# The head of a two-block kernel on one core: three units of the first projection multiplied together, their input loaded ahead of the fourth half of weights, squares on ScalarE

## The reference, cut to what matters

```python
def rmsnorm(x, g):
    xf = x.astype(jnp.float32)
    y = xf * lax.rsqrt(jnp.mean(xf * xf, axis=-1, keepdims=True) + EPS)
    return (y * g.astype(jnp.float32)).astype(x.dtype)
...
        z = rmsnorm(h, norm1_g[l])
        proj = z @ w_in[l]
        u_pool = proj[..., :POOL_WIDTH]
        x_lru = proj[..., POOL_WIDTH:POOL_WIDTH + LRU_WIDTH]
        g_lru = proj[..., POOL_WIDTH + LRU_WIDTH:]
```

## Time and profile before

| | before |
|---|---|
| median of 3 runs | 3289.7 us (3287.39 to 3292.03) |
| the profiled execution's own time | 3288.59 us |
| its span, first to last instruction | 3286.8 us |
| TensorE busy | 3185.9 us (97%) |
| VectorE busy | 2188.5 us (67%) |
| ScalarE busy | 1691.0 us (51%) |
| GpSimd busy | 806.1 us (25%) |
| mean granted TensorE clock | 0.988 |

### The profile page before, as it was taken

One profiled execution on the slowest core, in us unless ns is written; L12 is line 12 of the kernel. 1 busy time (PEld: TensorE's weight loads), 2 busy tenths in 40 slices (PEclk: granted clock), 3 DMA queues, 4 the chain that ended last, 5 costly groups with the idle time before them and its releaser, 6 DMA issues.

```text
span 3286.8 us, 46958 instructions
## 1 busy us (share of the span) xinstructions
PE 3185.9 (97%) x18222; PEld 2777.5 (85%) x18222; DVE 2188.5 (67%) x2908; ACT 1691.0 (51%) x2625; POOL 806.1 (25%) x782
## 2 busy tenths in 40 slices
PE   7999989999999999999999998999999899999998
PEld 6788878888888888888888887888888788888887
DVE  7757999864655555555646569999675865555564
ACT  5554457644545444454545655565657444444454
POOL 1332321321312222231313434222351200000003
PEclk9999999999999999999999999999999899999999
DMA  6465546666565656666666554555666466666664
GB/s 213 150 199 180 178 160 221 234 188 212 186 213 187 213 186 212 186 211 186 186 211 186 187 184 141 159 162 175 190 189 189 148 189 189 191 189 190 191 188 140
DMA packets 177709, 615.35 MB, mean 187 GB/s; under 512 B 18128, under 2 KB 34896, under 8 KB 176080
## 3 DMA queue, kind: packets, MB, share of 16 engines
q1 hardware_dynamic: 157824, 572.59, 55.1%
q10 hardware_dynamic: 19664, 39.76, 3.4%
HBM read 593.41 MB, written 18.87 MB: 186 GB/s over the span
## 4 chain that ended last, share of the span: by engine, by line
PE 74%; DVE 15%; issue 4%; ACT 3%; POOL 3%; DMA 1%; ACTq 0%; DVEq 0%; POOLq 0%
PE G L404 49%; PE G L405 25%; DVE lo L1002 6%; DVE CV L1305 2%; POOL tS L1487 1%; DVE oneB L1280 1%; ACT hi L631 1%; DVE oneA L1282 1%; DVE tS L1008 1%; ACT oneB L808 0%; DVE ZA L1328 0%; POOL X L1507 0%; POOL acc L1512 0%; DVE oneB L1285 0%; DMA X<-in_xT 0%
## 5 line engine op out<-in xcount | busy, mean ns | idle before, releaser
L404 PE MATMUL G<-ZA,hi 128*128 128x512 f32 x5120 | 1821.7, 400 | 29.4 <-DVE lo L1002 11.7
L1002 DVE TENSOR_TENSOR lo<-raw,hi 128x1024 fp32r<-128x1024 f32 x1088 | 1436.9, 1342 | 305.5 <-ACT hi L631 305.0
L405 PE MATMUL G<-ZA,lo 128*128 128x256 f32 x5120 | 1437.9, 281 | 0.0
L404 PE MATMUL G<-ZB,hi 128*128 128x512 f32 x3568 | 1250.2, 396 | 5.9 <-DVE ZB L1293 4.9
L404 PEld LDWEIGHTS G<-ZA,hi 128*128 128x128 f32 x5120 | 969.1, 189 | 261.9 <-DVE lo L1002 13.6
L631 ACT ACTIVATE hi<-raw 128x1024 fp32r<-128x1024 f32 x1088 | 1115.5, 1051 | 65.9 <-DMA raw<-in_pv 37.8
L405 PE MATMUL G<-ZB,lo 128*128 128x256 f32 x3584 | 1001.6, 279 | 0.0
L405 PEld LDWEIGHTS G<-ZA,lo 128*128 128x128 f32 x5120 | 973.8, 190 | 0.4
L404 PEld LDWEIGHTS G<-ZB,hi 128*128 128x128 f32 x3568 | 669.6, 188 | 167.5 <-DVE lo L1002 3.3
L638 ACT ACTIVATE tA<-G 128x256 f32<-128x256 f32 x559 | 212.4, 380 | 974.2 <-PE G L405 973.3
L405 PEld LDWEIGHTS G<-ZB,lo 128*128 128x128 f32 x3584 | 676.2, 189 | 0.0
(11 more groups left out here) (270 smaller groups left out, 1363.2 us busy)
## 6 DMA issues: line engine op xcount, KB each, us to landing
raw<-in_pu SPq DMA_DIRECT2D x256, 512.0 KB, 3.6
raw<-in_pv SPq DMA_DIRECT2D x256, 512.0 KB, 3.9
raw<-in_w_in SPq DMA_DIRECT2D x192, 512.0 KB, 3.5
raw<-in_w_up SPq DMA_DIRECT2D x128, 512.0 KB, 3.8
raw<-in_w_down SPq DMA_DIRECT2D x128, 512.0 KB, 4.2
raw<-in_w_out SPq DMA_DIRECT2D x32, 512.0 KB, 3.5
raw<-in_wq SPq DMA_DIRECT2D x32, 512.0 KB, 3.5
g_scratch<-stage ACTq DMA_DIRECT2D x16, 1024.0 KB, 4.8
```

The lines of the kernel that those rows point to most:

```text
L404: pe.matmul(G[:, 0:512], hi[h % NW][:, k % 8, :], Z[:, k, :], start=first, stop=False, skip_group_check=True)
L405: m = pe.matmul(G[:, 0:256], lo[h % NRAW][:, k % 8, :], Z[:, k, 0:256], start=False, stop=last, skip_group_check=True)
L1002: dve.tensor_tensor(lo[r][:, :, :], raw[r][:, :].rearrange("p (k n) -> p k n", k=8), hi[w][:, :, :].bitcast(F32), ALU.subtract).then_inc(s ...
```

## The change

1. `PAIRS` becomes `GROUPS`, and units 0, 1 and 2 become a group of three: the order of their halves is now (0,0) (1,0) (2,0) (0,1) (1,1) (2,1), and TensorE multiplies, for each k, unit 0, 1 and 2 in turn, into three banks. The wait for a half's weights now stands at its own first pair.
2. SyncE issues three halves of weights, then waits until the third piece of x (k = 5 to 9) has landed, and issues the others after it.
3. The 16 columns of g1 are loaded by themselves (8 KB) behind the first piece of x; the other 522 columns follow after the last piece of x.
4. ScalarE and VectorE split the weight halves at other places between the pieces of x (`SPLIT_X`): halves 0 and 1 behind k = 0, half 2 behind k = 1, halves 3, 4, 5 behind k = 7, half 6 behind k = 15.
5. The squares are four instructions of 1024 columns on ScalarE. VectorE adds eight squares in three steps, of 1024, 512 and 256 columns, twice, in place of two reduces.
6. Units 0 to 3 are evacuated later: the joins of 0 and 1 at u = 3, the rest of them and unit 2 at u = 4, units 3 and 4 at u = 5. `total` stands behind unit 3, and the gates behind units 5 (two), 6 (one), 7 (two), 8 (two) and 9 (one).
7. The loads of the gate weights are issued at u = 2 and not at u = 0.

```diff
 DNB = [M0 + 16 + 32 * c for c in range(4)]
-PAIRS = (VB[0], M0)
+GROUPS = {LX: 3, VB[0]: 2, M0: 2}
+INSIDE = [g + n for g, c in GROUPS.items() for n in range(1, c)]
 OUT_ORDER = (6, 7, 4, 5, 2, 3, 0, 1)
...
 for _u in range(N):
-    if _u in PAIRS:
-        HALVES += [(_u, 0), (_u + 1, 0), (_u, 1), (_u + 1, 1)]
-    elif _u - 1 not in PAIRS:
+    if _u in GROUPS:
+        HALVES += [(_u + _n, _p) for _p in range(2) for _n in range(GROUPS[_u])]
+    elif _u not in INSIDE:
         HALVES += [(_u, 0), (_u, 1)]
...
-    held = {0: 2, WQ: WQ + 2, F0: F0 + 3, F0 + 1: F0 + 3}
+    held = {0: 4, 1: 4, 2: 4, 3: 5, WQ: WQ + 2, F0: F0 + 3, F0 + 1: F0 + 3}
     return [w for w in range(max(0, u - 3), min(u, N)) if held.get(w, w + 1) == u]
...
-    return [h for h in ((3, 4, 5, 6) if u == 0 else (2 * u + 5, 2 * u + 6)) if h < NH]
+    return [h for h in ((6,) if u == 0 else (2 * u + 5, 2 * u + 6)) if h < NH]
...
+GATES_AT = {5: (0, 1), 6: (2,), 7: (3, 4), 8: (5, 6), 9: (7,)}
+SPLIT_X = {0: (0, 1), 1: (2,), 7: (3, 4, 5)}
 TAIL_END = [7, 13, 18, 22]
...
             for h, (u, p) in enumerate(HALVES):
+                if h == 3:
+                    sp_.wait_ge(s_x[2], 16)
                 if h >= NRAW:
...
-            def pair(u):
-                for w in (u, u + 1):
+            def group(u):
+                units = range(u, u + GROUPS[u])
+                for w in units:
                     bank_free(BANK[w])
                 for p in range(2):
-                    for w in (u, u + 1):
-                        weights_ready(POS[w][p])
                     for n, k in enumerate(range(8 * p, 8 * p + 8)):
                         operand_ready(u, k)
-                        for w in (u, u + 1):
+                        for w in units:
+                            if n == 0:
+                                weights_ready(POS[w][p])
                             product(w, p, n, k, GB[BANK[w] % 4], p == 0 and n == 0, p == 1 and n == 7)
...
                     break
-                if u in PAIRS:
-                    pair(u)
-                elif u - 1 not in PAIRS:
+                if u in GROUPS:
+                    group(u)
+                elif u not in INSIDE:
                     half(u, 0)
...
                     half(u, 1)
-                if u == 1:
-                    pe.wait_ge(s_con, 16)
-                    total(0, tQ[0], tQ[1], (s_fs, 1), (s_fs, 2)).then_inc(s_mean, 1)
                 if u == 3:
-                    gates(0)
-                    gates(1)
-                if 4 <= u < 10:
-                    gates(u - 2)
+                    pe.wait_ge(s_con, 32)
+                    total(0, tQ[0], tQ[1], (s_fs, 3), (s_fs, 6)).then_inc(s_mean, 1)
+                for j in GATES_AT.get(u, ()):
+                    gates(j)
                 if u in (11, 13, 15, 17):
...
                 halves = []
+            if u == 3:
+                evac(0, 1)
+                evac(1, 1)
+            if u == 4:
+                for n in (0, 1):
+                    evac(n, 2)
+                    evac(n, 3)
+                    if n == 0:
+                        prep(halves[0])
+                units, halves = [2], halves[1:]
             if len(units) > 1:
...
                 if i == 0:
-                    act.dma_start(col[:, :], ins["cols"]).then_inc(s_col, 16)
+                    act.dma_start(col[:, 0:16], ins["cols"][:, 0:16]).then_inc(s_g1, 16)
+            act.dma_start(col[:, 16:NCOL], ins["cols"][:, 16:NCOL]).then_inc(s_con, 16)
             act.dma_start(con[:, :], ins["con"][:, 0:CEND]).then_inc(s_con, 16)
-            for i in range(4):
-                act.wait_ge(s_x[i], 16)
-                if i == 0:
-                    act.wait_ge(s_col, 16)
-                for k in range(xcut[i], xcut[i + 1]):
-                    act.activation(ZA[:, k, 0:256], X[:, k, :], ACT.Copy, scale=C("g1", k)).then_inc(s_zxh, 1)
-                if i != 2:
-                    prep((0, 1, None, 2)[i])
+            act.wait_ge(s_g1, 16)
+            for k in range(16):
+                if k in xcut:
+                    act.wait_ge(s_x[xcut.index(k)], 16)
+                act.activation(ZA[:, k, 0:256], X[:, k, :], ACT.Copy, scale=C("g1", k)).then_inc(s_zxh, 1)
+                for h in SPLIT_X.get(k, ()):
+                    prep(h)
+            def squares(i):
+                act.activation(sqx[:, 4 * i:4 * i + 4, :], X[:, 4 * i:4 * i + 4, :], ACT.Square).then_inc(s_sqx, 1)
+            squares(0)
+            squares(1)
             for u in range(N + 1):
...
                 if u == 0:
+                    squares(2)
+                    squares(3)
+                if u == 2:
+                    act.wait_ge(s_con, 32)
                     act.dma_start(ry["gaw"][:, :, :], ins["gaw"]).then_inc(s_gw, 16)
                     act.dma_start(ry["gxw"][:, :, :], ins["gxw"]).then_inc(s_gw, 16)
-                if u == 1:
+                if u == 3:
                     act.wait_ge(s_mean, 1)
...
                     act.dma_start(ry["poolw"][:, :, :, :], ins["poolw"]).then_inc(s_poolw, 16)
-                    gates(0)
-                    gates(1)
+                for j in GATES_AT.get(u, ()):
+                    gates(j)
                 if u == 5:
...
                     act.activation(sp4[:, 0, :], sp4[:, 0, :], ACT.Ln, bias=1.0).then_inc(s_spa, 1)
-                if 4 <= u < 10:
-                    gates(u - 2)
                 if u in (9, 10):
...
             dve.memset(warm[:, :], 0.0).then_inc(s_warm, 1)
-            for i in range(4):
-                for k in range(xcut[i], xcut[i + 1]):
-                    dve.wait_ge(s_zxh, k + 1)
-                    dve.scalar_tensor_tensor(out=ZA[:, k, 256:512], in0=X[:, k, :], scalar=C("g1", k),
-                                             in1=ZA[:, k, 0:256].bitcast(F32), op0=ALU.mult, op1=ALU.subtract).then_inc(s_zx, 1)
-                if i != 2:
-                    prep((0, 1, None, 2)[i])
-            dve.tensor_tensor(gpp[:, :], col[:, COL0["gpost"]:COL0["gpost"] + 16],
-                              col[:, COL0["gpmlp"]:COL0["gpmlp"] + 16], ALU.mult).then_inc(s_gpp, 1)
+            for k in range(16):
+                dve.wait_ge(s_zxh, k + 1)
+                dve.scalar_tensor_tensor(out=ZA[:, k, 256:512], in0=X[:, k, :], scalar=C("g1", k),
+                                         in1=ZA[:, k, 0:256].bitcast(F32), op0=ALU.mult, op1=ALU.subtract).then_inc(s_zx, 1)
+                for h in SPLIT_X.get(k, ()):
+                    prep(h)
+            def squares_sum(p):
+                dve.wait_ge(s_sqx, 2 * p + 2)
+                for n, w in enumerate((4, 2, 1)):
+                    a, b = sqx[:, 8 * p:8 * p + w, :], sqx[:, 8 * p + w:8 * p + 2 * w, :]
+                    if n:
+                        dve.wait_ge(s_fs, 3 * p + n)
+                    dve.tensor_tensor(a if w > 1 else tQ[p][:, :].unsqueeze(1), a, b, ALU.add).then_inc(s_fs, 1)
             taps = 0
...
                     gate_split(VB.index(u), 0)
-                if u == 0:
-                    dve.wait_ge(s_sqx, 3)
-                    dve.tensor_reduce(tQ[0][:, :], sqx[:, 0:8, :].rearrange("p k t -> p t k"), AX.X, ALU.add).then_inc(s_fs, 1)
                 walk(u, evac, prep)
...
                     gate_split(VB.index(u), 1)
-                if u == 0:
-                    dve.wait_ge(s_sqx, 4)
-                    dve.tensor_reduce(tQ[1][:, :], sqx[:, 8:16, :].rearrange("p k t -> p t k"), AX.X, ALU.add).then_inc(s_fs, 1)
+                if u in (0, 1):
+                    squares_sum(u)
+                if u == 2:
+                    dve.wait_ge(s_con, 32)
+                    dve.tensor_tensor(gpp[:, :], col[:, COL0["gpost"]:COL0["gpost"] + 16],
+                                      col[:, COL0["gpmlp"]:COL0["gpmlp"] + 16], ALU.mult).then_inc(s_gpp, 1)
                 if u == 61:
                     decode()
-                if u == 1:
+                if u == 3:
                     dve.wait_ge(s_root, 1)
...
                 pool.memset(b[:, :, 0:16], 0.0).then_inc(s_pad, 1)
-            for i in range(4):
-                k = slice(xcut[i], xcut[i + 1])
-                pool.wait_ge(s_x[i], 16)
-                pool.tensor_tensor(sqx[:, k, :], X[:, k, :], X[:, k, :], ALU.mult).then_inc(s_sqx, 1)
             for u in range(N + 1):
```

8 lines of the change are left out of this document (4 added, 4 removed).

## The result

| | before | after |
|---|---|---|
| median of the runs made together | 3287.64 us (5 runs, 3286.53 to 3292.03) | 3272.12 us (5 runs, 3269.59 to 3277.6) |
| ratio, 95% interval | | 0.9958 [0.9943, 0.9973] |
| the profiled execution: time, span | 3288.59, 3286.8 us | 3272.12, 3270.3 us |

A forecast was written before the change was run, and what follows sets the result against it. TensorE, 97% busy of 3286.8 us, loses 27.2 us in the head to waits and its lower clock. Work before unit 4 ends at 36.2 instead of 50.31: 14.1 us off 3288.59 gives 3274.5, 3275.6 by median, stated 3275; range 3271 to 3282.

The forecast's parts named there:

- The likeliest case: Whole kernel: gain of 14.1 us, stated as 3275 us, own range 3272 to 3278 us; chance 0.70.
- Start: Head, first loads and splits: g1 lands at 6.2 us, `lo2` is done and TensorE runs without a pause from 11.8.
- Clock: First eight k: TensorE's clock rises 4.4 us into unbroken work; 7 pairs at 0.64 us until 16.3, 15 at 0.35.
- Loads of weights: Head: halves 3 to 7, issued at 10.4 us, land at 14.3, 16.0, 17.6, 18.9 and 20.2.
- weights too late: Second eight k: half 5 lands at 22 us, not 17.6, and the clock may fall back; gain 10, 3279 us; chance 0.10.
- slower: Head: SyncE's wait holds back weights from half 3 on; half 5 lands at 40, 6.6 us slower, 3296 us; chance 0.03.
- Second eight k, unit 3, total: Head on TensorE: 24 pairs end at 29.9 us, then 16 pairs and 0.7 for `total` end at 36.2, sums hidden.
- The join of unit 0: VectorE: joins of units 0 and 1 end at 35.9 and 36.3 us; unit 4 needs unit 0's bank at 36.2.
- Root and reciprocal: Behind `total`: mean there at 36.2 us, root at 37, reciprocal of 1.74 us from 38.7 until 40.5.
- the backlog shows: VectorE's reciprocal and all convolutions 3 to 5 us late through ScalarE's root; gain 9 to 11, 3279 us; chance 0.08.
- The gain isn't kept: Pooling stage: VectorE is the bound there and fills the time up, 3283 to 3295 us; chance 0.05.
- Rule against row, the reduce: VectorE's sums: were three adds as slow as a reduce, convolutions come 3.1 us later, unit 6's gates wait 3; gain 11.

The follow-up runs named there:

- run 6: Changed kernel with all of `col` loaded as one transfer behind the first piece of x: 3270.41 us, one run.
- run 7: Changed kernel with the g1 slice issued ahead of the first piece of x: 3270.78 us, one run.
- run 10: Changed kernel with the gate weights' loads moved behind the root (u = 3), the pooling weights a step later: 3265.72 us, one run.
- run 5: Changed kernel without SyncE's wait for the third piece of x: 3265.5 us, one run.
- run 3: Changed kernel with the two reduces of eight squares back in place of the six adds: 3280.43 us, one run.
- run 9: Changed kernel with 18 matmuls of zeros on TensorE ahead of the first pair: 3278.48 us, one run.
- run 12: The changed kernel unedited, run again on one chip beside the combined kernel: median 3269.5 us (12 runs), ratio to before 0.9953.
- run 8: Changed kernel with weight halves 0 and 1 split ahead of k = 0 on ScalarE and VectorE: 3275.32 us, one run.
- the combined kernel: Changed kernel with the edits of run 5, run 7, run 8, run 9 and run 10 together: median 3273.01 us (12 runs), ratio to before 0.9967.
- run 4: Changed kernel with the squares back on GpSimd, four pieces as they land: 3283.04 us, one run.

## Why the prediction was right, and where its steps were off

The forecast was 14.1 us at unit 4, 3275 us in all; measured were 13.4 us at unit 4, 12.9 at the mark, and a ratio worth 13.8. The likeliest case came true, and none of the rivals at its size. The median of 3272.12 us is 2.9 under the 3275 that I named, less than single times of one kernel differ by. Of the 1.3 us by which the mark came later than forecast (78.15, not 76.9), 0.7 were there at unit 4 (36.92, not 36.2) and 0.5 were lost behind it. Step by step:

- **Start.** `col`'s g1 piece was there at 7.50, not at 6.2, near the end of the bounds that the Trainium skill's rule had spoken for. The step took a value between its bounds for so few bytes; what counts more is the place behind 128 KB of x (runs 6 and 7). `lo2` was done at 12.9 in place of 11.8: 1.1 us. The prediction speaks of a queue that x and the weights share. They have two, ScalarE's and SyncE's; what they share is the bandwidth of the loads.
- **Clock.** I had it rise at 16.3, 4.4 us behind the start of the run; it rose 3.2 us behind it, at 16.1. Four pairs and a half instead of seven at the lower clock gave 0.5 us back. This was luck: in the twelve profiles that have such a start the time to the first pair of 0.36 us lies between 3.2 and 5.3 us (4.6 in the kernel before). It was 3.2 and 4.0 in the two profiles of the changed kernel and 5.3 in run 10, where this part is the same; with 5.3 the gain at `total` would have been 1 us less.
- **Loads of weights.** Half 3 was there at 15.56 (forecast 14.3), the halves 4 and 5 at 16.85 and 18.13 (16.0, 17.6). `lo5` was done at 20.45, k = 8 near 20.8, and TensorE came to it at 22.1: 1.3 us of the slack of 1.7 that the rival *weights too late* had to use up was left. SyncE's wait, which this rival and *slower* hung on, makes half 5 1.2 us later, but TensorE doesn't feel it (run 5).
- **Second eight k, unit 3, total.** 40 pairs from 22.1 end at 36.25, 0.353 us each, as worked out. The three adds took 2.4 us (26.41 to 28.80), forecast 2.3. The second sums were ready at 33.40, and `total` wanted them at 36.68.
- **The join of unit 0** ended near 36.1, and its bank was wanted at 36.92. I gave this place one clause. It has 0.8 us of slack, the least ahead of unit 4, and it is what the reduces (run 3) and the earlier start (run 9) run into.
- **Root and reciprocal** came at 39.93 and 40.44, 2.9 and 1.7 us later than forecast. Of this, 1.3 us go with half 12, which was loaded beside the gate weights (run 10). About 1.1 are the end of `total`, which was near 37.3 and not at 36.2. The rest is a term that I had too small: ScalarE loads a table for the root, 1.28 us from 38.64, and I had allowed 0.8 in all from the mean to the root. Before, that load stood at 27.32, long ahead of the mean. A late root is the mechanism of *the backlog shows*. The step had the convolution of unit 6 done at 68.4 and its gates at 68.5. VectorE's and TensorE's timelines have them at 70.46 and 70.60, just behind the gates of unit 5 (69.59, 0.87 us long), so this chain was at its limit; in run 12, the same program with `total` 0.3 us sooner, TensorE waits for it:

```profile
68.93 1.53 DVE L1072 SCALAR_TENSOR_TENSOR XC<-XL,col,XC 128x256 f32<-128x256 f32 x3
...
70.60 0.67 PE L455 MATMUL M<-XC,gaw 128*128 128x256 f32 x2
```

```profile
70.28 0.67 PE L455 MATMUL M<-XC,gaw 128*128 128x256 f32 x2 [0.36 <-DVE XC L1072]
```

  In runs 7 and 8 this wait is 0.40 and 0.19 us. So the backlog did show, for 0.1 to 0.4 us and not for the 3 to 5 of the rival, and one of the signs named as proof against me, a wait of TensorE for a convolution, is there. The step "I take no wait, and at most 2 us" holds by its second half. In run 10, and in the combined kernel, whose root is at 37.1, there is no such wait.
- **Kept.** The 12.9 us pass unchanged to 188 us. *The gain isn't kept* was wrong on the place that it named. Between unit 4 and the mark 0.5 us of the 13.4 are lost, and TensorE's timeline says where. The wait at 70.6 costs 0.2 (the two gates there take 1.76 us, elsewhere 1.54). The other 0.4 are of the new places of the gates: two that stand together take 1.54 us (48.42 to 49.96), one alone 0.67 (55.80 to 56.47), and the change made two more such pairs of gates out of single ones. (The six units themselves came out 0.1 us shorter.) "All gates cost TensorE what they did" left this out.
- **Rule against row, the reduce.** With the reduces the price is 3.6 us; I had 3.1, by a wait at the gates of unit 6. The size was near, the mechanism another.

What each part is worth at the mark, of 12.9: the group 6.1, the squares off GpSimd 6.0, the adds 3.6. The g1 slice (0.7 in run 6) and SyncE's wait (0.2 in run 5) are within what the clock's rise moves. They add up to more than the whole since each is needed for the others.

**Open.** Why the time behind the head drifts between profiles (root R3 comes 1824 us behind the mark in run 5, 1834 in the changed kernel, 1841 in run 9) was not looked into. Nor was what decides between 3.2 and 5.3 us for the clock. The later evacuations and the new places of the gates were never undone by themselves, so that their price of 0.4 us is read from one timeline only.

## What to carry to other kernels

When TensorE starves because one operand is delivered piece by piece, multiply several units with each piece, and feed the weights of all of them first: one half of the change alone gave 0.9 us, the other 6.8, both 12.9. In a start-up, find the last operand that the first unbroken run of TensorE needs, and keep GpSimd from working beside VectorE until it is done; this was half of the gain. Judge such a change by one event at the end of the head, in the trace: 2 us are seen there, and in the whole time they are not. For less than that, measure from a later event to take the clock's rise out, as from `total` in run 10.

## What the runs showed of the hardware that I had not expected

- GpSimd's multiplications of SBUF tiles and VectorE's two-input instructions take turns: 1.22 becomes up to 3.76 us for 128x1024 and 0.47 becomes 2.54 for 128x256 on VectorE, and 1.89 becomes 2.87 for 128x1024 on GpSimd (run 4).
- A load of 8 KB lands only 0.2 to 0.8 us sooner than one of 269 KB at the same place in the queue, and put ahead of a load of 128 KB it makes that one land 5.6 instead of 3.7 to 4.2 us after its issue (runs 6 and 7).
- A start of TensorE that is 1 us earlier can be lost whole to a longer stretch at the lower clock (run 8); in three profiles of the same start that stretch was 3.2, 4.0 and 5.3 us; 10 us of matmuls on zeros ahead of it gave 2.4 GHz at once (run 9).
- Two gates together cost TensorE 1.54 us, and two alone 0.67 each.
- The unchanged kernel spreads by 24 us over 23 runs, 0.7%, with a mean clock of 0.987 to 0.989 in all.
